# Delta rule's short convolution: the first of four taps on ScalarE instead of VectorE

## The reference

```python
def gated_deltanet_group(qkv, z, b_raw, a_raw, sc_w, A_log, dt_bias, norm_w):
    bsz, seq, _ = qkv.shape
    qkv = jax.nn.silu(causal_depthwise_conv(qkv, sc_w))
    q = qkv[..., :GDN_WIDTH].reshape(bsz, seq, GDN_HEADS, HEAD_DIM)
    k = qkv[..., GDN_WIDTH:2 * GDN_WIDTH].reshape(bsz, seq, GDN_HEADS, HEAD_DIM)
    ...
    q, k = l2norm(q), l2norm(k)
    ...
    o = chunk_gated_delta_rule(q, k, v, g, beta)
```

## Time and profile before

| what | value |
|---|---|
| median of three executions | 3379.43 us (3379.13 to 3382.83) |
| the profiled execution, its own time | 3380.5 us |
| its span, first to last instruction | 3378.4 us |
| TensorE matmul busy | 3347.8 us, 99% of the span |
| VectorE busy | 2162.8 us, 64% |
| ScalarE busy | 1640.4 us, 49% |
| mean granted TensorE clock | 0.998 |
| the six `qkv` tiles' drains | 1108.3 to 1264.5 us |

### The profile page before, as it was taken

One profiled execution on the slowest core, in us unless ns is written; L12 is line 12 of the kernel. 1 busy time (PEld: TensorE's weight loads), 2 busy tenths in 40 slices (PEclk: granted clock), 3 DMA queues, 4 the chain that ended last, 5 costly groups with the idle time before them and its releaser, 6 DMA issues.

```text
span 3378.4 us, 44895 instructions
## 1 busy us (share of the span) xinstructions
PE 3347.8 (99%) x17588; PEld 2840.8 (84%) x17588; DVE 2162.8 (64%) x2819; ACT 1640.4 (49%) x1945; POOL 6.3 (0%) x9
## 2 busy tenths in 40 slices
PE   8999999999999999999999999999999999999998
PEld 7887888888888998888888888898898888888887
DVE  6777655555567997664444566777775644457666
ACT  4445544444444455544444465544554455555554
POOL 0000000000000000000000000000000000000000
PEclk9999999999999999999999999999999999999999
DMA  6555566666655633656666666656556555566554
GB/s 198 149 163 156 154 193 198 197 202 202 216 174 167 176 112 88 210 170 191 188 190 189 192 213 194 182 162 176 162 148 214 170 187 183 189 207 202 193 194 156
DMA packets 324237, 608.74 MB, mean 180 GB/s; under 512 B 28317, under 2 KB 42655, under 8 KB 322792
## 3 DMA queue, kind: packets, MB, share of 16 engines
q1 hardware_dynamic: 317704, 587.46, 57.2%
q10 hardware_dynamic: 6368, 19.01, 1.5%
HBM read 604.29 MB, written 2.10 MB: 179 GB/s over the span
## 4 chain that ended last, share of the span: by engine, by line
PE 91%; DVE 5%; ACT 2%; issue 1%; DMA 1%; SPq 0%; ACTq 0%; DVEq 0%
PE ps L667 25%; PE ps L669 25%; PE ps L668 25%; PE ps L702 7%; PE ps L710 3%; DVE w_lo L2074 1%; DVE arena L2080 1%; DVE xtok L2080 1%; ACT w_hi L1473 1%; DMA ring<-in_w_in 1%; PE ps L682 0%; PE ps L938 0%; PE ps L909 0%; PE ps L1078 0%; SPq L581 0%
## 5 line engine op out<-in xcount | busy, mean ns | idle before, releaser
L2074 DVE TENSOR_TENSOR w_lo<-ring,w_hi 128x1024 fp32r<-128x1024 f32 (+2 forms) x1136 | 1368.7, 1209 | 1056.1 <-ACT w_hi L1473 876.4
L1473 ACT ACTIVATE w_hi<-ring 128x1024 fp32r<-128x1024 f32 (+2 forms) x1136 | 1184.4, 1047 | 1464.1 <-PE ps L667 1294.3
L667 PE MATMUL ps<-w_hi,x_both 128*128 128x512 f32 (+1 forms) x2272 | 891.7, 392 | 1.1 <-DVE w_lo L2074 0.9
L669 PE MATMUL ps<-w_hi,x_both 128*128 128x512 f32 (+1 forms) x2272 | 876.9, 386 | 0.0
L668 PE MATMUL ps<-w_lo,x_both 128*128 128x512 f32 (+1 forms) x2272 | 876.4, 386 | 0.0
L667 PEld LDWEIGHTS ps<-w_hi,x_both 128*128 128x128 f32 x2272 | 427.3, 188 | 88.2 <-issue 10.1
L669 PEld LDWEIGHTS ps<-w_hi,x_both 128*128 128x128 f32 x2272 | 427.3, 188 | 82.8
L668 PEld LDWEIGHTS ps<-w_lo,x_both 128*128 128x128 f32 x2272 | 427.7, 188 | 77.7 <-issue 0.5
L667 PE MATMUL ps<-w_hi,h_hi 128*128 128x512 f32 x864 | 336.6, 390 | 0.0
L669 PE MATMUL ps<-w_hi,h_lo 128*128 128x512 f32 x864 | 336.5, 390 | 0.0
L668 PE MATMUL ps<-w_lo,h_hi 128*128 128x512 f32 x864 | 336.5, 389 | 0.0
(11 more groups left out here) (361 smaller groups left out, 3060.4 us busy)
## 6 DMA issues: line engine op xcount, KB each, us to landing
ring<-in_w_in SPq DMA_DIRECT2D x416, 512.0 KB, 3.7
ring<-in_w_down SPq DMA_DIRECT2D x216, 512.0 KB, 4.5
ring<-in_w_gate_up SPq DMA_DIRECT2D x176, 512.0 KB, 3.7
ring<-in_w_up SPq DMA_DIRECT2D x128, 512.0 KB, 4.3
ring<-in_w_out SPq DMA_DIRECT2D x64, 512.0 KB, 4.4
ring<-in_w_branch SPq DMA_DIRECT2D x36, 512.0 KB, 4.3
ring<-in_w_in SPq DMA_DIRECT2D x48, 384.0 KB, 3.2
ring<-in_w_o SPq DMA_DIRECT2D x32, 512.0 KB, 4.7
```

What stands on the lines that cost most here:

```text
L667: first = pe.matmul(out, left[0], right[0], start=start, stop=False)
L669: return first, pe.matmul(out, left[1], right[0], start=False, stop=stop)
L1473: last = act.activation(w_hi[:, s, :, 0:width], ring[:, s, :, 0:width], ACT.Copy)
L2074: return dve.tensor_tensor(o, a, b, op)
```

## The change

After the drain of each `qkv` tile ScalarE waits for its own write, multiplies the four groups by the first tap (Copy with a column as scale) into `c_qkv` and raises a new semaphore, `first_tap`. VectorE's slot for the first tap is empty; its three other taps wait for `first_tap` instead of the drain.

```diff
                 act.activation(c_raw[:, u, :, RP:RP + S], ps[:, 2 * u:2 * u + 2, :].rearrange("p a (c s) -> p (a c) s", c=2),
                                ACT.Copy).then_inc(tile_free[u], 1)
+                act.wait_ge(tile_free[u], sec.taken(t)[1])
+                for c in range(4):
+                    last = act.activation(c_qkv[:, 4 * t + c], c_raw[:, u, c, 0:S], ACT.Copy, scale=scw[:, 0, 4 * t + c:4 * t + c + 1])
+                last.then_inc(first_tap, 1)
...
-                        for k in range(SHORT_W):
+                        for k in range(1, SHORT_W):
                             if at == Slots.SHORT + 16 * t + 2 * k:
                                 short_step(t, k)
...
-                sec = plan["qkv"]
-                u, count = sec.taken(t)
-                dve.wait_ge(tile_free[u], count)
+                u = plan["qkv"].taken(t)[0]
+                dve.wait_ge(first_tap, t + 1)
                 for c in range(4):
                     o, r, wk = c_qkv[:, 4 * t + c], c_raw[:, u, c, k:k + S], scw[:, k, 4 * t + c:4 * t + c + 1]
-                    last = tsc(o, r, wk, ALU.mult) if k == 0 else stt(o, r, wk, o, ALU.mult, ALU.add)
+                    last = stt(o, r, wk, o, ALU.mult, ALU.add)
```

More of the change, by code:

```diff
@@ L368, in build @@
         staged, turned, conv_rows_ready = sem("staged"), sem("turned"), sem("conv_rows_ready")
-        cross_out, gate_silu, up_whole, relu_done = (sem(k) for k in ("cross_out", "gate_silu", "up_whole", "relu_done"))
+        cross_out, first_tap, relu_done = (sem(k) for k in ("cross_out", "first_tap", "relu_done"))
         wide_order = sem("wide_order")
```

## The result

The changed kernel takes 3387.58 us (median of 13 executions, 3384.16 to 3390.57), the kernel before 3379.64 us beside it (3379.13 to 3382.83): ratio 1.0021, 95% interval 1.0014 to 1.0028. That is 7.9 us more by the two medians and 7.1 us by the ratio. The forecast was 3384.3 us, 4.9 us more, in a range of 3380.0 to 3388.5. The kernel is slower by about the 0.2% that was taken as the bound; measured once more, with other runs of the kernel before, the ratio was 1.0018 (1.0009 to 1.0027), 3387.39 against 3380.61 us.

What follows compares the result with a forecast made beforehand. TensorE, busy 3347.8 of 3378.4 us, was taken as the bound, so only its waits or slow running count. Path 3.7 plus clock 1.2 gave 4.9 us over 3379.43, 3384.3 us; range 3380.0 to 3388.5, the forecast's own part 1 to 6.7 more.

Steps and rivals of the forecast that it cites:

- the clock rival: TensorE's clock falls at sums of squares of tiles 0 to 2 and once more: 7.3 us more, 3386.7; chance 0.29.
- dear taps: ScalarE's four taps per tile at the two-column price, 2.08 us; with the clock rival 9.1 us more, 3388.5.
- the path: Drain, short convolution, SiLU, square, sums of squares: longer by 3.7 us in all as felt by TensorE, tiles 0 to 4.
- the clock: TensorE falls to half clock behind longer waits at sums of squares: one fall more than before, 1.2 us.
- The taps' price: Four first-tap products on ScalarE take 1.72 us a tile; not excluded were 2.08 and VectorE's own price, 1.14.
- w_lo 2.74 us after the drain: VectorE's first `w_lo` of the next tile begins 2.74 us after ScalarE's drain ends, behind taps and `w_hi`.
- Waits of 3.7 to 4.3 us at L1188: Sign of being right: TensorE waits for squares at all four tiles, 3.7 to 4.3 us instead of 1.3.
- No wait in the ring: TensorE does not wait for delayed `w_lo` in the weights' ring, which has 4 us of cover: no cost.
- engine against engine: Comparing only tap prices on ScalarE and VectorE: path 0.58 us longer a tile, some 1.5 us in all.
- four or more stretches at clock 0.50: Sign of being wrong: TensorE's trace shows at least four stretches at the lower clock level, 1.2 GHz.
- the 1.9 us wait of L682 brought no fall: Evidence that a fall is not sure: TensorE's longer, later wait, untouched by the change, left the clock up.
- The relief: VectorE, freed of the first tap, shortens the path; waits of 1.9 us vanish, with one fall 3.1 us gained; chance 0.11.

Runs made afterwards that it cites:

- e6_tile5_only: Kernel before with the first tap moved to ScalarE for tile 5 alone, VectorE keeping it for tiles 0 to 4: 3379.47 us, ratio 1.0001 to the kernel before.
- e1_split_first: The change, with ScalarE making the next tile's first `w_hi` ahead of the four taps instead of behind them: 3378.07 us, ratio 0.9991 to the kernel before.
- e8_block_behind: Kernel before, VectorE keeping all taps, plus four unused ScalarE products behind the next tile's first `w_hi`: 3379.02 us, ratio 0.9997.
- e10_change_again: The change itself, unaltered, measured and traced once more: 3387.39 us (3384.02 to 3390.25).
- e3_filler: The change plus two unused TensorE products ahead of the wait for each tile's squares, at four places: 3383.03 us, ratio 1.0007 to the kernel before.
- e1 to e6: Includes three without own line: before plus idle ScalarE products ahead of `w_hi`, 3389.21 us; change plus the same, 3403.1; before plus TensorE fillers, 3382.16.
- e7: Kernel before with the first tap moved to ScalarE for tile 1 alone: 3381.54 us, ratio 1.0005 to the kernel before.
- e9: The kernel with the first `w_hi` ahead of ScalarE's taps, measured again beside the change: 3378.33 us, ratio 0.9992 to the kernel before.

## Why the prediction was right

The measured 7.9 us (7.1 by the ratio) stand against a forecast of 4.9. The range held the result, but by its upper end, which was the clock rival's with dear taps; the forecast's own 1 to 6.7 us lay below it. What was right is the path, and what was too small is the clock.

**The path** was right, tile by tile. The first trace of the change has no fall between its drains, and e6_tile5_only is, up to tile 5, the kernel before without one:

| tiles | before, no fall | change, no fall | more | forecast |
|---|---|---|---|---|
| 0 to 1 | 25.62 | 25.98 | 0.36 | 0.39 |
| 1 to 2 | 24.81 | 26.00 | 1.19 | 1.08 |
| 2 to 3 | 26.79 | 27.80 | 1.01 | 0.94 |
| 3 to 4 | 33.23 | 33.92 | 0.69 | 0.71 |
| 4 to 5 | 44.43 | 44.93 | 0.50 | 0.6 |
| sum | | | 3.75 | 3.7 |

- *The taps' price* of 1.72 us for four, taken from L1575, was 1.71 (one took 0.494). The dear price of two columns and the cheap one of VectorE's own product did not come.
- *w_lo 2.74 us after the drain*: 2.72.
- *Waits of 3.7 to 4.3 us at L1188*: 3.4, a little under the sign.
- *No wait in the ring*: right; TensorE never waits at L667 in this stretch, in the changed kernel either.
- *Part of tile 3's share earlier, at the head products*: right, L1211 has a wait of 0.20 us there and one of 0.20 us at tile 4.
- *Order decides, not engine*: the advice of the Trainium skill, page "ScalarE: Activation LUTs", section "Rules for kernel authors", priced engine against engine, came to some 1.5 us; the measured path is 3.75, and with the same engine and another order it is gone (e1_split_first, e8_block_behind). So the measurement decides against pricing engine against engine here.

**The clock** was mis-sized. The step of the prediction that failed is "I count one fall more than before: 1.2 us". Two things in it were too small. One stretch of 3.4 us at half clock costs not 1.2 but 1.46 us: in the trace of before tile 3's drain and tile 4's are 34.69 us apart with one fall, 33.23 in e6_tile5_only without:

```profile
1185.58 1.03 ACT L1978 ACTIVATE ln_gb<-ps 128x1024 f32<-128x1024 f32 x1 [1.12 <-PE ps L669]
...
1218.81 1.03 ACT L1978 ACTIVATE ln_gb<-ps 128x1024 f32<-128x1024 f32 x1 [1.12 <-PE ps L669]
```

And in e10_change_again the clock stayed down twice as long, some 6.8 us, at each of the two places where it fell, 3.06 us a place. An execution of the change without a fall would take about 3382.7 us, by estimate: the first trace's 3384.16 less the 1.6 of its fall behind L682, or e3_filler's lower seven, 3382.66 to 3383.15. The medians of 3387.4 and 3387.6 lie 4.8 us over that. The kernel before has its lower executions at 3378.3 to 3379.2 and medians of 3380.5 to 3380.7 in its larger sets, some 1.8 over. The clock's part is the difference, by this estimate about 3.0 us, instead of 1.2. Path and clock give 6.8 us; the two pairs of medians lie 6.8 and 7.9 apart (in the second the kernel before stood at 3379.64, in 13 executions).

The prediction named "four or more stretches at clock 0.50" as a sign that it was wrong. Up to the kernel's end, where TensorE has no more work, the change's first trace has one stretch of 3.4 us. The trace of e10_change_again has three places: twice some 6.8 us behind squares and once 3.4 behind L682, which is five stretches by length. So in that trace the sign came. And "the 1.9 us wait of L682 brought no fall" held for the trace of before only: behind this wait, which the change does not touch, the clock fell in 8 of the 12 traces (in the change's two, in e1 to e6; not in before, e7, e8, e9). It costs 1.6 us: from ScalarE's drain ahead of L682 to a pair of its copies 100 us later are 102.15 us in the change's first trace, with the fall (first fence), and 100.54 in that of before, without it:

```profile
1362.64 1.00 ACT L1989 ACTIVATE ln_gb<-ps 128x1024 f32<-128x1024 f32 x1
...
1464.79 1.09 ACT L1535 ACTIVATE x_both<-ps 128x512 fp32r<-128x512 f32 x2 [3.04 <-PE ps L884]
```

```profile
1360.35 1.00 ACT L1985 ACTIVATE ln_gb<-ps 128x1024 f32<-128x1024 f32 x1
...
1460.89 1.09 ACT L1535 ACTIVATE x_both<-ps 128x512 fp32r<-128x512 f32 x2 [3.06 <-PE ps L884]
```

**The rival** "the clock falls at nearly every wait" had the right size, 7.3 us, but not quite its mechanism: the trace of e10_change_again shows two of four places, at more than double the price. How many fall in the median execution no run shows, since only two executions of the change were traced. The rival had 0.29, and the forecast's own 1 to 6.7 us 0.57; by size the measurement lies in the rival's part, just over the border.

**The relief** was rightly given little: it wins only once `w_hi` no longer stands in the way, and then 2.1 us of path and 2.3 to 2.7 us in the medians, where 1.9 and, with one fall, 3.1 had been reckoned for it.

The two profiled executions alone would have misled about the size: they lie 3384.16 - 3380.5 = 3.7 us apart. Each has one fall of 3.4 us, before's behind tile 3's square and the change's behind L682, so what is left between them is the path.

## What to carry to other kernels

Before moving work to an idle engine, read what stands behind the place where it is put, and who waits for that: here 1.7 us of ScalarE's idle time sat exactly between two links of a chain that TensorE waits for, and one place later the same work was free, and its relief of VectorE was worth 2.1 us. Price a wait of TensorE by its length and by what it does to the clock behind it; next to nearly empty products a wait of 0.9 us cost up to 3 us more. Where medians move and traces do not agree with them, compare the distances between the same instructions in two executions whose times differ, over the whole trace and not only in the part that was changed.

## What the runs showed of the hardware

A wait of under 1 us ahead of eight one-column products was enough for the clock to go to its lower level, and not in every execution: in the change's first trace, with waits of 0.91, 0.92, 0.77 and 0.82 us, it fell at none of the four places, in e10_change_again, with the same waits to 0.01 us, at two. Behind the wait of some 1.9 us at L682, the same in every trace, it fell in 8 of 12. What decides between falling and not falling these traces do not show. The Trainium skill, page "TensorE: Matmul & The Clock Gate", section "What's actually happening", says that the clock follows how busy TensorE has recently been; the rows agree, and e3_filler agrees most: drains as far apart as in the change's first trace to 0.02 us, two useless products in each wait, and a median 4.5 us lower.

A stretch at half clock does not cost half of its length on TensorE: 0.42 to 0.47 us for each us here (1.46 and 1.61 of 3.4, 3.07 of some 6.8, 4.34 of 10.24, the last with the price of the four products taken off).
